# A fused two-block network on one core: sixteen modulation products move from TensorE to ScalarE and GpSimd

## The reference, cut to what matters

```python
mod = (silu(c) @ w_ada + b_ada)               # (1, 1024) @ (1024, 6144)
sh1, sc1, ga1, sh2, sc2, ga2 = jnp.split(mod, 6, axis=-1)
h = rmsnorm(x, ln1_pre) * (1.0 + sc1) + sh1
proj = h @ w_in                               # the first projection, 512 x 2816
```

## Time and profile before

| what | value |
|---|---|
| time before, median of 3 runs | 2185.94 us (2184.53 to 2190.42) |
| the profiled execution, its own time | 2187.34 us |
| its span in the profile | 2185.5 us |
| `win1` and what runs beside it | 47.66 to about 346 us of the span |
| TensorE busy in the span | 1910.1 us (87%) |
| ScalarE / GpSimd busy in the span | 551.9 us (25%) / 475.8 us (22%) |

### The profile page before, as it was taken

The page is one execution under the profiler, slowest core; times in us unless marked ns, Lnnn a source line. Parts: engine busy times, 40 slices in busy tenths (PEclk is TensorE's granted clock), DMA queues, the critical chain, the costliest instruction groups (busy, mean ns, idle before and its releaser), DMA issues.

```text
span 2185.5 us, 32417 instructions
## 1 busy us (share of the span) xinstructions
PE 1910.1 (87%) x13222; PEld 1296.8 (59%) x13223; DVE 858.6 (39%) x1997; ACT 551.9 (25%) x1026; POOL 475.8 (22%) x523
## 2 busy tenths in 40 slices
PE   5999998759878279899999989899999999999766
PEld 3777787635433168678766657645565555556432
DVE  3154534353221422521477432334444534443226
ACT  4242512311101431412477412201111211111111
POOL 1000000023221100000345000004444544454320
PEclk9998999879999689979999999889999999999998
DMA  8665521359999451211477322348999999999977
GB/s 323 238 244 178 208 117 58 144 195 413 417 418 397 158 141 53 87 23 55 110 147 168 79 105 88 124 174 340 384 405 358 409 407 376 383 381 399 358 281 307
DMA packets 102472, 527.33 MB, mean 241 GB/s; under 512 B 28002, under 2 KB 28306, under 8 KB 48172
## 3 DMA queue, kind: packets, MB, share of 16 engines
q1 hardware_dynamic: 63216, 451.70, 52.3%
q0 software_dynamic: 36256, 64.54, 10.8%
q10 hardware_dynamic: 2844, 8.85, 1.2%
HBM read 519.36 MB, written 51.90 MB: 261 GB/s over the span
## 4 chain that ended last, share of the span: by engine, by line
PE 71%; DMA 16%; DVE 7%; ACT 3%; issue 2%; SPq 0%; POOL 0%; ACTq 0%; POOLq 0%; DVEq 0%
PE ps L251 31%; PE ps L1738 16%; DMA arena<-in_egu 11%; PE ps L1812 8%; DMA arena<-in_ada 3%; PE ps L1704 2%; PE ps L411 2%; PE ps L2942 1%; PE ps L1799 1%; PE ps L433 1%; PE ps L2968 1%; PE ps L2254 1%; DMA arena<-in_bs_row 1%; PE ps L1073 1%; DMA arena<-y_rows 1%
## 5 line engine op out<-in xcount | busy, mean ns | idle before, releaser
L1738 PE MATMUL ps<-arena 128*64 128x256 f32 x4096 | 484.1, 391 | 63.6 <-DMA arena<-in_egu 52.3
L1738 PEld LDWEIGHTS ps<-arena 128*64 128x64 f32 x4096 | 300.2, 141 | 272.0 <-issue 75.8
L251 PE MATMUL ps<-arena 128*128 128x256 f32 (+4 forms) x1268 | 325.3, 418 | 3.3 <-ACT arena L3092 0.9
L251 PEld LDWEIGHTS ps<-arena 128*128 128x128 f32 (+1 forms) x1268 | 228.0, 204 | 84.1 <-issue 63.6
L1686 POOL DMA_INDIRECT arena<-h_rows,arena x160 | 192.2, 1201 | 297.4 <-DVE arena L1667 133.4
L1692 POOL DMA_INDIRECT y_rows<-arena x160 | 160.5, 1003 | 404.7 <-DVE arena L1843 347.2
L1812 PE MATMUL ps<-arena 128*64 128x512 f32 x1024 | 242.2, 602 | 6.5 <-DVE arena L1807 2.5
L1807 DVE COPY arena<-ps 128x256 f32<-128x256 f32 (+1 forms) x96 | 36.5, 380 | 432.8 <-PE ps L1799 432.8
L1786 ACT ACTIVATE arena<-ps 128x256 f32<-128x256 f32 (+1 forms) x96 | 33.5, 349 | 518.6 <-PE ps L1738 518.6
L2906 POOL DMA_DIRECT2D arena<-in_nabias x160 | 85.5, 542 | 356.9 <-PE ps L2771 200.1
L302 DVE TENSOR_TENSOR wlb<-arena,whb 128x1024 fp32r<-128x1024 f32 (+1 forms) x46 | 55.7, 1212 | 195.7 <-ACT whb L294 195.7
(11 more groups left out here) (429 smaller groups left out, 2776.3 us busy)
## 6 DMA issues: line engine op xcount, KB each, us to landing
arena<-in_egu SPq DMA_DIRECT2D x204, 1024.0 KB, 13.4
arena<-in_ed SPq DMA_DIRECT2D x102, 1024.0 KB, 9.6
arena<-in_ada SPq DMA_DIRECT2D x48, 1024.0 KB, 7.0
arena<-in_win SPq DMA_DIRECT2D x33, 1024.0 KB, 5.1
arena<-y_rows SPq DMA_DIRECT2D x20, 1024.0 KB, 13.7
arena<-in_nabias POOLq DMA_DIRECT2D x96, 128.0 KB, 5.6
arena<-in_wout SPq DMA_DIRECT2D x8, 1024.0 KB, 7.2
h_rows<-arena ACTq DMA_DIRECT2D x8, 512.0 KB, 3.6
```

Of the source, the lines that this page charges most:

```text
L251: z = pe.matmul(o, l, r, start=start and i == 0, stop=stop and i == len(pairs) - 1, skip_group_check=check)
L1738: z = pe.matmul(b[64 * j:64 * j + 64, 256 * s:256 * s + 256], XV[:, c, 64 * h:64 * h + 64], wk(k)[:, j * 256:j * 256 + 256], start=k == 0, ...
```

## The change

Of products 4 to 23, those in `ON_POOL` (4 to 11 and 16 to 23, sixteen of them) are no longer done by TensorE. ScalarE multiplies each of the 16 weight blocks of a product, 128x256 and in place, by a per-partition column of the vector. GpSimd then adds the 8 blocks of a slot in three steps (4 blocks, 2 blocks, 1 block wide), the last one into `MS[n % 2]`. TensorE's fold multiplies by `ones` in place of `SEL` for these. Products 12 to 15 stay on TensorE: they belong to the second block. All folds move later by one turn: in piece (p, q), p at least 1, the fold is of product 2 + 2p + q, two behind, and the folds of 22 and 23 come in pieces (10,0) and (10,1). VectorE's bias additions move with them. Every fold now also waits for `ROWS`.

For products 16 to 23 the scaling column is of `c_2` alone, so both output columns of their fold hold that sum; nothing later reads the second column of these products.

```diff
-            if n not in (0, 2, 4):
-                pe_ada_fold(pe, w, n - 1, order)
-            if n in (1, 3, 23):
-                pe_ada_fold(pe, w, n, order)
+
+        ON_POOL = [n for n in range(4, 24) if not 12 <= n < 16]
...
+        def act_scaled(act, w, n):
+            for i in range(2):
+                s = ring.of(ada, "w", n, i)
+                wv = cut(s.ap, 8)
+                w.wait_ge(*s.landed)
+                for k in range(8):
+                    c = MC1[:, k:k + 1] if PAIRS[n][0] == 0 else mc2v[:, k, 0:1]
+                    z = act.activation(wv[:, k, :], wv[:, k, :], ACT.Copy, scale=c)
+                z.then_inc(*ada.up("act", "scaled", n, i))
+
+        def pool_ada(pool, w, n):
+            w.wait_ge(*ada.to("fold", n - 2))
+            for i in range(2):
+                wv, acc = cut(ring.of(ada, "w", n, i).ap, 8), MS[n % 2][:, 256 * i:256 * i + 256]
+                for k in (4, 2):
+                    w.wait_ge(*(ada.to("scaled", n, i) if k == 4 else ada.to("part", n, i, 4)))
+                    pool.tensor_tensor(wv[:, 0:k, :], wv[:, 0:k, :], wv[:, k:2 * k, :], ALU.add).then_inc(*ada.up("pool", "part", n, i, k))
+                w.wait_ge(*ada.to("part", n, i, 2))
+                pool.tensor_tensor(acc, wv[:, 0, :], wv[:, 1, :], ALU.add).then_inc(*ada.up("pool", "mm", n, i))
...
-            w.wait_ge(*ada.to("ms", n))
+            w.wait_ge(*(ada.to("mm", n, 1) if n in ON_POOL else ada.to("ms", n)))
+            w.wait_ge(*ld.to(*ROWS))
...
-                z = pe.matmul(b.ap[:, c * width:(c + 1) * width], MS[n % 2][:, c * 128:(c + 1) * 128], SEL[:, 0:width],
-                              start=True, stop=True)
+                z = pe.matmul(b.ap[:, c * width:(c + 1) * width], MS[n % 2][:, c * 128:(c + 1) * 128],
+                              ones[:, 0:width] if n in ON_POOL else SEL[:, 0:width], start=True, stop=True)
...
-                    if n:
-                        pe_ada(pe, w, n, KVB if (p, q) == (9, 1) else AB)
+                    if n and n not in ON_POOL:
+                        pe_ada(pe, w, n, AB)
+                    if p:
+                        pe_ada_fold(pe, w, 2 + 2 * p + q, KVB if p == 10 or (p, q) == (9, 1) else AB)
...
                     if n:
-                        act_ada(act, w, n)
+                        (act_scaled if n in ON_POOL else act_ada)(act, w, n)
...
-                    if p < 9 and n > 4:
-                        dve_ada(dve, w, n - 1)
+                    if 0 < p < 9:
+                        dve_ada(dve, w, n - 2)
...
+            for n in ON_POOL:
+                pool_ada(pool, w, n)
             pool_xa(pool, w)
```

More of the change, by code:

```diff
@@ L651, in pe_start @@
                 pe_ada(pe, w, n, first)
+                if n:
+                    pe_ada_fold(pe, w, 0, first)
+                    pe_ada_fold(pe, w, 1, first)
             w.wait_ge(*ld.to(*VECS))
@@ L657, in pe_start @@
                 pe_ada(pe, w, n, first)
+            for n in (2, 3):
+                pe_ada_fold(pe, w, n, first)
         def act_start(act, w):
@@ L894, in dve_win1 @@
                         else:
-                            dve_ada(dve, w, 21)
+                            dve_ada(dve, w, 20)
                             for m in range(4):
@@ L898, in dve_win1 @@
                     elif (p, q) == (9, 1):
-                        for k in (22, 23):
-                            dve_ada(dve, w, k)
+                        dve_ada(dve, w, 21)
                         for m in range(4, 8):
@@ L903, in dve_win1 @@
                     elif p == 10:
+                        dve_ada(dve, w, 22 + q)
                         for m in range(8, 12) if q == 0 else range(12, 16):
```

## The result

The changed kernel takes 2236.97 us in the median of 4 runs (2232.37 to 2242.46), the kernel before 2185.24 us in the same set of runs. The ratio is 1.0238, 95% interval 1.0204 to 1.0272: **52 us slower**. The profiled execution took 2232.37 us.

The account below looks back on a forecast made before the run. TensorE was taken to bound the stage before, the two weight slots to set the rate after. First run 28, second run 8 and clock 2 make 38 us on the 2185.9 median: 2224, range 2198 to 2252.

Parts of the forecast that it names:

- The wheel: Two in_ada slots: each round is transfer, scaling, sums, next transfer; 13.25 us per product, bounds 9.4 and 15.3.
- The first run: Products 4 to 11: slot rounds delay product 12 on TensorE, so (4,1) starts at 168.3, 28 us later.
- rival 2: VectorE and GpSimd delay each other: 8 us more over seven rounds, some 4 in the second run; 2236; chance 0.20.
- The sum's price: GpSimd's sums: 2.2 ns an element, 4.35 us per half with starts and waits, bounds 2.0 and 5.1.
- Transfers: Weight transfers into the in_ada slots, starting a half apart: 5.5 us, where 4.8 is best and 7.0 the median.
- The hand-back: At product 12, done by TensorE, its lead of two turns is given back; (4,1) comes 28 us later.
- The second run: Products 16 to 23: ScalarE's scalings delay exps, squares and root, so pe_head and spread wait; together 8 us.
- What TensorE waits for in the first run: TensorE idles some 6 us in front of each fold up to 160 us, released by GpSimd; longest before product 12.
- Rival 3: Pauses of 12 us at (8,0) and (8,1) put two more pieces at 1.2 GHz, 5.7 us each; 2235; chance 0.12.
- rival 1: Cheap sums, 2.0 us a half: round 10.9, (4,1) 8 us late, ScalarE's order still costs 7; 2201; chance 0.11.
- rival 4: Faster: slots keep up, TensorE's saving stays, needs sums of 1.1 us a half; 2151 to 2175; chance 0.03.
- rival 5: It cancels: cheap sum and short transfer, (4,1) 4 us early, against ScalarE's 8 less the folds; within 0.3%; chance 0.03.

Follow-up runs that it names:

- e10: Changed kernel with GpSimd doing only the last of three sums per half; later stages on other data, no total; (4,1) starts at 144.7 us.
- e5: Changed kernel with the four products that stay on TensorE put first, the sixteen moved ones behind: 2213.7 us, ratio 1.0136.
- e3: Changed kernel with only products 16 to 23 on ScalarE and GpSimd, 4 to 11 back on TensorE: 2200.33 us, ratio 1.0103.
- e2: Changed kernel with only products 4 to 11 on ScalarE and GpSimd, 16 to 23 back on TensorE: 2222.06 us, ratio 1.0211.
- e9: Kernel before with two extra weight slots alone, old order of folds, nothing moved: 2182.38 us, ratio 0.9990.
- e6: Changed kernel with a product's scalings moved to the end of ScalarE's turn, behind exps, squares and root: 2241.95 us, ratio 1.0283.
- e4: Changed kernel with four weight slots for products 4 to 11, the two new ones in idle tiles: 2202.34 us, ratio 1.0098.
- e1: Changed kernel with all 20 products back on TensorE, only the later order of folds and bias additions kept: 2185.01 us, ratio 1.0028.
- e12: Changed kernel with only products 16 and 17 moved, late folds kept: 2187.09 us against 2184.74 before, ratio 1.0013.

## Why the prediction was right, point by point

- **The direction and the mechanism held.** Forecast 2224, range 2198 to 2252, measured 2237. The wheel is in the chain of waits, spoke by spoke. Its round was forecast at 13.25 us and is 13.7: transfer 4.9 (forecast 5.5), scaling 3.3 (3.1), sums 5.3 in the half that the chain goes through (4.35). The size fell short: 38 us forecast, 52 measured.
- **The first run: 28 us forecast, 36 measured.** The whole trace after starts `win1` 1.7 us earlier, so (4,1) is 174.4 + 1.7 - 140.3 = 35.8 us late. Of the 8 us more, 2.6 are in product 4 (its second half ends at 67.9 + 1.7 against 67.0), 2.2 in five rounds of 13.68 in place of 13.25, 2.3 in the last two rounds (29.3 together), 0.9 between the slot and (4,1). Cut by cause: in the sums that the chain goes through, what goes beyond 2.43, 1.31 and 0.73 us is 0.9 in product 4, 0.8 in each of the five rounds, and 2.8 in the last two (256 elements took 2.65 and 1.60 us in place of 0.73), 7.9 us in all, each time with a VectorE operation beside it. The rest cancels: sums and scalings a little dearer, ScalarE's exp, table loads and Silu in the last rounds (5.8 us between two scalings, 0.5 allowed), against shorter transfers. So the term mis-sized is GpSimd's half, and the most of it is that the sum put VectorE's part at nothing and left it to rival 2.
- **The sum's price.** 2.43 us for 1024 elements, 1.31 for 512 and 0.73 for 256 with VectorE still: 0.2 us and 2.2 ns an element. The element's price, taken between the rows' bounds, was right; a half with VectorE still is 4.5 us and 0.1 between the sums, near the 4.35. The Trainium skill (GPSIMD Engine Reference, Performance versus the Vector engine) gives 4497 ns for 2048 elements, from which one estimates the same 2.2 ns; the trace agrees. Sums were the one price that no row gave, and e10 shows how much hung on it: 30 us.
- **Transfers** at 4.9 us were better than the 5.5 allowed, because they seldom overlap now. This hid some of the miss.
- **The hand-back.** That the lead of two turns is lost at product 12 was the step by which slack would not save the change. e5 agrees: 20 us less with another order, though it changes more than this. In e3, which has no hand-back, the eight products of the second run cost 22 us, in e2, which has it, the eight of the first 44.
- **The second run: 8 us forecast, 13 measured** from (4,1) to the end. The two places named, `pe_head` in (8,0) and the spread in (8,1), are where TensorE waits, 15.1 and 8.0 us. The reason was half right. The forecast had ScalarE's order alone; in the trace product 19 also waits for its slot, behind GpSimd's sums and a transfer, and when the sums are nearly gone (e10) 7 or 8 us go and 6 (15 against e9) stay. The other order tried, e6, is no cure.
- **What TensorE waits for in the first run was told wrong in one detail.** I expected it in front of each fold, released by GpSimd. So it was for the first two (3.8 and 4.1 us); from (3,0) on it waited in front of the fold for VectorE's softmax step (11.4 us), which stood behind the rounding, which stood behind ScalarE's wait for `in_ada`. The same wheel, one engine further off.
- **Rival 2 (contention)** came true beside the forecast's mechanism: some 0.85 us of a half when it strikes, and more in the last rounds, 7.9 us over the first run where rival 2 had 8. Its 2236 is the measured time, the forecast's own 2224 is 13 us short of it. Against the whole 52 us it is the smaller part (e4 takes 28 away and leaves it in place). No run takes contention away and leaves the sums, so its price is read from the trace alone. The remainder's own 9.6 us more (20 x 0.48) lie mostly beside waits.
- **Rival 3 (half clock):** the clock fell as the earlier trace rows suggested, to 0.78 on average from 50 to 120 us and 0.71 to 174. (4,1)'s projection took 10.1 us, in e1 7.5. It cost little where the wheel covered it, as assumed. After the pauses at (8,0) and (8,1) the clock was at 0.50 from 290 to 296 us and from 310 to 316, then full; half of such a stretch, an estimated 3 us, is the price of each, where rival 3 had 5.7.
- **Rivals 1, 4 and 5** needed a cheap sum, of 2.0 us a half or less. It was 4.96; e10, with 0.78 us of sums in a half, is the case they describe, and there (4,1) came at 144.7, between the 148 that rival 1 gives and the kernel before. Its sums are also below the 1.1 us at which rival 4 had (4,1) on time, and (4,1) was still 4 us late.
- **What stays open.** The extra 9.6 us at half clock in the profile of the kernel before stand between 178.8 and 230.8 us, in the part that "8 forecast, 13 measured" compares. Against e9, whose time can't be told from that of the kernel before, the second run costs 212.4 - 189.7 = 22.7 us, which is what e3 measured (21.9), and the whole stage 386.8 - 329.9 = 56.9 in place of 47. The 52 us of the medians lie between. How often either kernel has such a stretch, a single profile of each doesn't tell. Behind the stage nothing was slower in these executions: from the issue of the expert weights to the end (own time less the last column of the table) they took 1845.6 us in the changed kernel, 1847.9 in the kernel before and 1848.3 in e9.

## What to carry to other kernels

Before moving work off the busiest engine, follow the buffer, not the engine: write down the round from "slot free" over transfer, every new pass and back, and hold it against the pace of the consumer. Two slots and three serial steps on three engines give the sum of the steps, however idle the engines are. And lateness that is hidden by running ahead must be kept to the end: where the old, direct path comes back behind the new one, it comes out there. None of the versions tried beats the kernel before; the best moved version (e12) can't be told from it.

## What the runs showed that I had not expected

- A GpSimd sum and a VectorE operation with two inputs hold each other up when they meet: 2.48 us in place of 1.225 for VectorE's, 4.58 in place of 3.72 for GpSimd's two, and 2.65 in place of 0.73 for one of 256 elements. VectorE's copy of the cost vanished when only the 256-element sums were left (1225 ns).
- TensorE's clock after nearly the same pause (2.9 us) was 1.2 GHz in the profile of the kernel before and 2.4 GHz in e1's, 4.7 us apart in one piece. A comparison of two single profiles at the level of 5 us needs a look at the granted clock first.
- Two more slots took 28 of the 52 us away, with every operation as before, and gave the kernel before nothing (ratio 0.9990): the same resource was slack in one kernel and the bound in the other.
